# RMS-norm at the head of a hybrid RWKV-7 / short-conv / expert block: a diagonal matrix of reciprocal roots on TensorE, in place of VectorE's scaling and TensorE's transposes

## The reference

```python
def _rmsnorm(x, g):
    y = xf * lax.rsqrt(jnp.mean(xf * xf, axis=-1, keepdims=True) + NORM_EPS)
    return (y * g)

h = concat([meta, x])                        # (1040, 1024)
x_n = _rmsnorm(h, ln1_g)                     # the stage that the change touches
proj = x_n @ w_in                            # r, k, v, conv parts, two gates
y_a = _rwkv7_branch(x_n, pr, pk, pv, ...)    # token shift, low-rank decay/a/g, delta-rule scan over 1040 steps
y_b = _short_conv_branch(cb, cc, ch, ...)
h = h + (sigmoid(gate_a) * y_a + sigmoid(gate_b) * y_b) @ w_o
h = h + _moe(_rmsnorm(h, ln2_g), ...)        # top 4 of 32 experts, clamped SwiGLU
out = _rmsnorm(h, lnf_g)[16:]
```

## Time and profile before

| | us |
|---|---|
| median of 3 runs | 2727.32 |
| lowest and highest of them | 2718.69, 2734.62 |
| the profiled execution, its own time | 2717.3 |
| its span | 2715.7 |

### The profile page before, as it was taken

One profiled execution on the slowest core, in us unless ns is written; L12 is line 12 of the kernel. 1 busy time (PEld: TensorE's weight loads), 2 busy tenths in 40 slices (PEclk: granted clock), 3 DMA queues, 4 the chain that ended last, 5 costly groups with the idle time before them and its releaser, 6 DMA issues.

```text
span 2715.7 us, 61354 instructions
## 1 busy us (share of the span) xinstructions
PE 2555.9 (94%) x24101; PEld 2154.9 (79%) x24101; DVE 1736.5 (64%) x2053; ACT 1283.5 (47%) x1402; POOL 511.5 (19%) x593
## 2 busy tenths in 40 slices
PE   7898889898998999898999999999999999999995
PEld 5676767675998999788888888788878888888884
DVE  8657566564222112354677677676779999999996
ACT  3313131321221111242665666665667777777776
POOL 6000000000000000123433433433421111111111
PEclk9999989997999999998999999999999999999997
DMA  5000000000112112345777877877889999999999
GB/s 126 16 3 23 5 18 10 18 10 2 39 40 61 43 27 70 121 78 131 284 280 275 297 279 271 295 282 269 298 327 390 381 379 379 377 383 386 379 379 341
DMA packets 143110, 527.82 MB, mean 194 GB/s; under 512 B 18411, under 2 KB 72271, under 8 KB 91010
## 3 DMA queue, kind: packets, MB, share of 16 engines
q1 hardware_dynamic: 120642, 480.00, 47.4%
q0 software_dynamic: 22336, 45.93, 6.9%
HBM read 492.01 MB, written 33.86 MB: 194 GB/s over the span
## 4 chain that ended last, share of the span: by engine, by line
PE 86%; DVE 4%; DMA 3%; issue 3%; ACT 3%; POOL 0%; SPq 0%; ACTq 0%; DVEq 0%; POOLq 0%
PE bank L949 33%; PE bank L2215 13%; PE bank L2216 13%; PE bank L2217 13%; PE bank L2224 5%; DMA raw_first<-in_w_e_up 1%; PE bank L2187 1%; PE bank L2110 1%; DVE xmix L713 1%; PE bank L2256 1%; PE bank L2111 1%; PE bank L2112 1%; PE bank L2203 1%; PE bank L2162 1%; PE bank L2288 1%
## 5 line engine op out<-in xcount | busy, mean ns | idle before, releaser
L2018 DVE TENSOR_TENSOR w_lo<-raw_first,w_hi 128x2048 fp32r<-128x2048 f32 x267 | 601.9, 2287 | 107.7 <-ACT w_hi L1790 107.4
L1790 ACT ACTIVATE w_hi<-raw_first 128x2048 fp32r<-128x2048 f32 x268 | 515.9, 1925 | 227.3 <-DMA raw_first<-in_w_e_up 88.3
L2215 PE MATMUL bank<-w_hi,x_hi 128*128 128x512 f32 x1056 | 421.7, 399 | 4.2 <-ACT yo_rows L1842 4.2
L2217 PE MATMUL bank<-w_hi,x_lo 128*128 128x512 f32 x1056 | 413.2, 391 | 0.0
L2216 PE MATMUL bank<-w_lo,x_hi 128*128 128x512 f32 x1056 | 412.8, 391 | 0.0
L2018 DVE TENSOR_TENSOR w_lo<-raw_rest,w_hi 128x2048 fp32r<-128x2048 f32 x132 | 298.9, 2285 | 0.2
L1790 ACT ACTIVATE w_hi<-raw_rest 128x2048 fp32r<-128x2048 f32 x132 | 252.5, 1918 | 97.4 <-DMA raw_rest<-in_w_e_down 43.5
L949 PE MATMUL bank<-xm_hi,ring_hi 128*128 128x256 f32 (+1 forms) x896 | 260.3, 291 | 18.8 <-DVE dz L910 8.1
L949 PE MATMUL bank<-xnT,ring 128*128 128x260 f32 x880 | 246.8, 425 | 13.9 <-ACT pb L545 9.9
L949 PE MATMUL bank<-xm_hi,ring_lo 128*128 128x256 f32 (+1 forms) x896 | 254.1, 284 | 0.0
L949 PE MATMUL bank<-xm_lo,ring_hi 128*128 128x256 f32 (+1 forms) x896 | 253.0, 282 | 0.0
(11 more groups left out here) (380 smaller groups left out, 4150.3 us busy)
## 6 DMA issues: line engine op xcount, KB each, us to landing
raw_first<-in_w_e_up SPq DMA_DIRECT2D x134, 1024.0 KB, 7.1
raw_first<-in_w_e_gate SPq DMA_DIRECT2D x68, 1024.0 KB, 7.0
raw_rest<-in_w_e_gate SPq DMA_DIRECT2D x68, 1024.0 KB, 5.4
raw_first<-in_w_e_down SPq DMA_DIRECT2D x66, 1024.0 KB, 7.0
raw_rest<-in_w_e_down SPq DMA_DIRECT2D x66, 1024.0 KB, 8.5
ring<-in_w_in SPq DMA_DIRECT2D x40, 512.0 KB, 3.9
h_all<-in_x SPq DMA_DIRECT2D x8, 512.0 KB, 15.1
hn_d<-hn SPq DMA_DIRECT2D x8, 512.0 KB, 7.2
```

The costliest lines, as they stand in the source:

```text
L1790: nc.scalar.activation(w_hi[:, j % NRING, :, :], raw_piece(j), ACT.Copy).then_inc(hi_done, 1)
L2018: nc.vector.tensor_tensor(w_lo[:, j % NRING, :, :], raw_piece(j), w_hi[:, j % NRING, :, :].bitcast(f32), ALU.subtract).then_inc(lo_done, 1)
L2215: nc.tensor.matmul(ps[:, :], hi, w_hi[:, slot, k, :], start=start and k == 0, stop=False)
L2217: ins = nc.tensor.matmul(ps[:, :], lo, w_hi[:, slot, k, :], start=False, stop=stop and k == HK - 1)
```

## The change

The scaled tile `xn` goes away. VectorE multiplies the 104 by 104 identity with the column of reciprocals and so writes a diagonal matrix `dg`. TensorE multiplies the raw tile `x_in` (as weights) with `dg` (as moving operand), as an ordinary float32 matmul; before it transposed `xn`, with the identity as moving operand. The product is the scaled and transposed tile, in the same PSUM places. VectorE waits once for GpSimd's `ident` before its loop. `dg` takes the place of `xn` in SBUF, padded to the same size, so that no address behind it moves. The instructions stay in their order on every engine.

```diff
-    xn = s0("xn", [TP, 2, D])
+    dg = s0("dg", [TP, 2, TP])
+    s0.at += 4 * 2 * (D - TP)
...
+        dve.wait_ge(pool_c, 2)
         for t in range(NT):
             dve.wait_ge(std0_done, t + 1)
             nc.vector.reciprocal(rstd[:, t:t + 1], rstd[:, t:t + 1]).then_inc(rstd0_done, 1)
             dve.wait_ge(rstd0_done, t + 1)
             if t >= 2:
                 dve.wait_ge(xnT_ps, t - 1)
-            nc.vector.tensor_scalar(xn[:, t % 2, :], x_in[:, t, :], rstd[:, t:t + 1], None, ALU.mult).then_inc(xn_done, 1)
+            nc.vector.tensor_scalar(dg[:, t % 2, :], ident[0:TP, 0:TP], rstd[:, t:t + 1], None, ALU.mult).then_inc(xn_done, 1)
...
             for k in range(KT):
-                ins = nc.tensor.transpose(bank[2 * (t % 2) + k // 4][:, (k % 4) * TP:(k % 4 + 1) * TP],
-                                          xn[:, t % 2, 128 * k:128 * (k + 1)], ident[0:TP, 0:TP])
+                ins = nc.tensor.matmul(bank[2 * (t % 2) + k // 4][:, (k % 4) * TP:(k % 4 + 1) * TP],
+                                       x_in[:, t, 128 * k:128 * (k + 1)], dg[:, t % 2, :], start=True, stop=True)
             ins.then_inc(xnT_ps, 1)
```

## The result

| | before | changed |
|---|---|---|
| median of 20 runs each, us | 2728.89 | 2753.1 |
| mean (one run of 5079 us left out) | 2727.4 | 2749.4 |
| ratio of the runs, 95% interval | | 1.0066 [1.0041, 1.0092] |
| profiled execution, span | 2715.7 | 2764.4 |

The kernel became slower, by 0.7% by the ratio and by 22.0 us (standard error 3.9), 0.8%, by the means. The prediction, 2729.0 us (2716 to 2741) with 0.955 for no change, is wrong: the median of 2753.1 lies above its range. The runs of the kernel before also scatter more than the three that it had to go by, over 37 us (2710.14 to 2746.89) and not 16.

A forecast was written before the change was run, and what follows sets the result against it. TensorE holds 86% of the chain; the change acts only before `xmix`, where loads and VectorE's backlog set the pace. Walks of 37.5 against 35.9 us gave 1.7 us later: median 2727.3 to 2729.0 us, range 2716 to 2741.

The forecast's parts named there:

- The record's step at the low clock: First stage, TensorE: each new matmul record takes 0.181 us at the low clock, so a tile costs 2.90 us.
- The clock: First stage: TensorE never pauses in the first tiles, so its clock rises at about 15 us; records then take 0.107 us.
- the old stage had to stay low and the new one need not: First stage: transposes do not count as busy for TensorE's clock, so matmuls in their place could raise it.
- The low-clock rival: First stage: clock never rises, 2.90 us a tile, walk ends at 42.6, 6.7 us later, 2734.0 us; chance 0.22.
- The diagonal, the blocks, GpSimd: First stage: diagonals cost 0.2 us, two held by GpSimd's differences, which start at 19 and about 24 us; TensorE idles 3.4.
- The sum of the stage: First stage's end by walks: 37.5 us changed against 35.9 before, so 1.7 us later.
- the signs set down beforehand: Wrong if: `xmix` before 34 or after 41 us, steps over 0.2, no held diagonal, or time that `xmix` does not explain.
- Behind the stage everything moves with it: After the first stage: all later work shifts by the same delay as the start of `xmix`, 1.7 us.
- a shift: Later in the kernel: moved timing can add or take one clock drop, 1.7 us, put into the range.
- a matmul at four times a transpose: Rival, first stage: records cost twice the estimate, 5.8 us a tile, end at 68.8 us, 2760 us; chance 0.02.
- The rounds: Rival, from 1290 us on: different rounding changes experts and adds a round of about 43 us, 2770 us; chance 0.02.

The follow-up runs named there:

- e5: Changed kernel with the diagonal matrix 128 columns wide (24 of them zero) instead of 104; 2739.68 us.
- e1: Kernel before with only TensorE's transposes replaced by float32 matmuls with the plain identity, VectorE still scaling the tile; 2736.77 us, one run.
- e3: Changed kernel with five 512-column float32 matmuls on TensorE ahead of tile 0, to raise its clock; 2716.06 us.
- e17: Kernel before with eight dummy 256-column matmuls a pass, at the front's end and among the scan's `y` products; median 2700.26 us, ratio 0.9916.

## Why the prediction was wrong

**The record's step at the low clock (mis-sized).** "Scaled to 104 columns the steps are 0.174 [...] I take 0.181 us at the low clock." Measured 0.213. A sign of it was in hand, and I used it at one clock only: the router's matmuls have a floor that the moving columns don't explain, and it was read at full clock. (By the starts of single records it is 0.112 us and not 0.106, and a transpose's step is 0.173 and not 0.181: the first step of a group differs from the others, and my quotients took it in.) At the lower clock the floor is 0.213, 1.9 times as long. Scaling the keys' 260 columns down was right for the moving side alone. It costs (0.213 - 0.181) x 16 = 0.51 us a tile.

**The clock (failed).** "I expect the rise at about 15 us." It did not rise in the stage, in 20.81 us of unbroken matmuls, but only at 52.6 us, under the keys. The argument, that the keys' unbroken matmuls raised it, went from 260 columns a record to 104. In e5, with 128 columns, it rose at 14.6. Nor did "the old stage had to stay low and the new one need not" say what it seemed to: the changed stage has no transposes and stayed low as well, so these traces don't show that transposes are what kept the old one low. The low-clock rival, chance 0.22, is what happened; its walk ended at 42.6 with 2.90 us a tile, and ten tiles at 3.41 us add 5.1 to that, 47.7 against the 47.23 measured. Its time, 2734.0 us, was still 19 us short of the median.

**The diagonal, the blocks, GpSimd.** A diagonal costs 0.27 us (forecast 0.2), hidden. GpSimd's difference holds a small instruction too, as forecast: 3.70 us for one that otherwise takes 0.27. One diagonal was held in full, not two, since the first difference started just behind a diagonal (21.63 + 0.27 us) and TensorE was still supplied. A second one took 0.66 us, at the end of the first difference. The first difference started at 21.99 instead of 19, the second at 28.43 instead of 24, both behind TensorE. Behind the second TensorE idled 1.57 us, not 3.4.

**The sum of the stage.** 1.7 us forecast, 11.85 measured. By e1 all of it comes from the matmul's records; with a warm start (e3) 6.5 us remain, since the clock falls halfway. Of the signs set down beforehand three of those for "wrong" came: `xmix` behind 41 us, steps over 0.2 us, and a difference in time that `xmix` doesn't explain.

**"Behind the stage everything moves with it" (failed).** For a pure delay it is right within the error: 17.5 (4.4) for 13.5 us. I followed the waits and not the instruction stream. The 160 instructions moved the boundaries of all that follows, and 9.5 us of idle time and of clock drops went into the fronts; that the idle times are waits for the next block of instructions is inferred from how they move with the padding. The range allowed "a shift" one drop of 1.7 us; a drop at the start of a scan costs some 12 us (61.44 for the last scan of before, 49.86 in e17), since the clock then stays low for 30.7 us and more.

**What stands.** Means: 2727.4 to 2749.4 is 22.0 us; 11.85 is the stage, 9.5 the fronts, which leaves about 1 us for the scans, with an error of 4. The other two sets, 35.7 (6.0) and 18.1 (4.7), leave 14 and -3. The profiled execution of the changed kernel, 17 us above its mean, is the one with four low scans. What stays open is whether the shift makes low scans more frequent, why the clock stays low under the 104-column stream, and what sets the 0.213 us.

The other rivals: a matmul at four times a transpose is out (2 x 0.213 against 0.173 is 2.5 times at the low clock). The rounds are as before, since the part behind the passes differs by 0.8 us, and a round takes about 43.

## What to carry to other kernels

Price a matmul record by its moving columns and by the floor that records with few columns show, both at the clock that the stretch really has; here the floor was 0.112 us at the higher level and 0.213 at the lower. Take the lower level unless a stream of the same shape is seen to leave it. Read a step from the starts of single records, not from a group's length. When instructions are added to an engine, read also the idle times of "issue" in the stretches behind: a change at the head of a program can move them in a loop a hundred microseconds later, and a padded copy of the kernel before tells this from the change itself. Compare stretches rather than whole times where the scatter is larger than the effect. Where a serial chain of small matmuls scatters from run to run, look at its granted clock, and try a few dummy matmuls in its gaps: eight a pass gained 0.84% here by the ratio, 27.2 (2.6) us by the means, though part of that may be the moved boundaries.

## What was not expected of the hardware

- 104-column float32 matmuls with 128-column weights, unbroken for 20.81 us, stayed at the low level (0.213 us a record), and in none of seven profiles did the clock rise within the stage; with 128 moving columns the clock rose at 13.8 to 14.6 us (three profiles) and the records stepped by 0.112 us.
- TensorE had idle times of 0.5 to 1.9 us that no semaphore ends, at places that move with the number of instructions ahead. 160 more cost 9.5 us in the fronts of the four passes and took about 8 us of these idle times out of the scans; 256 more left both as they were.
- A scan step takes 0.90 us at the high level and 1.57 at the low one. Where the clock fell close to the start of a scan, and the scan became a low one, it stayed low for 30.7 to 41.0 us; other falls as close to one lasted 3.4 or 6.8 us, as the one 7.4 us ahead of the first scan of the kernel before (6.8 us).
- The granted clock read 1.00 throughout the first stage, though the records stepped at the low level. The trace's first clock event is the rise out of it: 41.6 us in the kernel before, 52.6 in the changed one, 14.6 in e5 and 8.0 in e3. Before the first event only the durations tell.
